# Split weight tiles and x tiles each followed by 16 unused bytes

## The chip, the cores and the metric

The kernel runs on one core of one Trainium2 chip. The metric is the device time of one execution, in microseconds (us). Three runs of the kernel before gave 2096.66, 2097.6 and 2097.91 us, median 2097.6 us.

## What is computed

One layer of a streaming encoder on 256 tokens of width 2048, in f32. Cut to its matrix products (names as in the kernel's stream):

```python
h = rmsnorm(x)                       # [256, 2048]
A, Z, GA..GC, BQK, BV, BO, CQK, CV = split(h @ w_in)       # three token mixers and their gates
x += (gate_a*(y_a@wb_a) + gate_b*(y_b@wb_b) + gate_c*(y_c@wb_c)) @ w_out     # BR, WO
q = rmsnorm(x) @ xa_wq;  k, v = split(rmsnorm(mem) @ xa_wkv)                 # Q, K, V
x += cross_attention(q, k, v) @ xa_wo                                        # XO
x += (silu(g) * u) @ ffn_down,  g, u = split(conv3(rmsnorm(x) @ ffn_up))     # UP, DN
```

The gated DeltaNet, the mLSTM and the stick-breaking attention between the products are not touched by the change.

## The kernel before, in words

Every large product is done in the format `float32r` with each operand split in two: a high part, the value rounded to that format, and a low part, the rest. Three matmuls replace one (function `three`, L1699): high weights by high x, high weights by low x, low weights by high x.

**Units and halves.** The stream (L43) cuts all weights into units of 256 columns. SyncE loads a unit into one of the two slots of `raw`. A unit is then worked on in two halves. ScalarE writes the high part of a half into `w_hi[:, half]` (L457, called from `hi_half`), VectorE writes `raw - w_hi` into `w_lo[:, half]` (L974, `lo_half`), and TensorE multiplies (`half_unit`, L1718). In the feature-major stages (kind FM and BR) a half is 16 blocks k of 128 rows by 128 columns, so 48 matmuls of 256 columns. The weights are the stationary operand there and x the moving one. In the down projection DN a half has 11 blocks, 33 matmuls. In UP (L1731 to L1737) the first two of the three products are one matmul of 512 columns, since the high and the low x are read in one access, so a half has 32 matmuls: 16 of 512 columns (L1735) and 16 of 256 (L1737). In the token-major stages BV, CV and V the roles are exchanged: x is stationary and 256 columns of weights move.

**Order.** TensorE takes the halves in the order of the stream. It waits for `lo_ready` before each, and ScalarE waits for `half_used` before it overwrites a half. Between the halves lie the smaller matmuls of the mixers and of the attention. The order is written out by hand.

**Where the tiles lie.** Tensors follow each other in each partition, each start rounded up to 32 bytes. In bytes modulo 128, counted from the start of `w_hi` (the place, below): `raw`, `w_hi` and `w_lo` have sizes that are multiples of 128, and so has a block of weights (512 bytes), so all blocks of weights lie at place 0. `x_home` starts at place 0 and the kernel puts x into it at a byte of its own for each use (L140): `x_hl` (all products with `w_in`) at 32, `x_wo` at 64, `x_q` at 96, `x_xo` at 16, `x_up` at 32. A block of x has 1024 bytes, and the low x lies 16384 bytes behind the high x, so the place is the same for all k and both parts. The tensors behind `x_home` add up so that `y_hl` (BR), `mem_hl` (K and V), `act_hl` (DN) and `gw_hi`, `gw_lo` (the four small gate matrices: 48 matmuls in the form of a half, after the first three halves of A) all lie at place 32.

In one table, with the relation, which is the place of the moving operand less that of the stationary one, modulo 128:

| products | moving | stationary | relation before |
|---|---|---|---|
| w_in, feature-major | x_hl, 32 | w, 0 | 32 |
| gate matrices | x_hl, 32 | gw, 32 | 0 |
| BR, K, DN | y_hl, mem_hl, act_hl, 32 | w, 0 | 32 |
| WO | x_wo, 64 | w, 0 | 64 |
| Q | x_q, 96 | w, 0 | 96 |
| XO | x_xo, 16 | w, 0 | 16 |
| UP | x_up, 32 | w, 0 | 32 |
| BV, CV, V | w, 0 | x_hl or mem_hl, 32 | 96 |

Of the kernel before, what the change touches and what calls it, by code (L numbers as in the profile page):

```python
# [8 lines left out]
P = 128  # L9
SEQ, D = 256, 2048  # L10
TT = SEQ // P
KC = D // P
# [7 lines left out]
CW = 256  # L20
# [95 lines left out]
def build_program(nc, T, out):  # L116
    f32, f32r = mybir.dt.float32, mybir.dt.float32r
    ALU, ACT, AX = mybir.AluOpType, mybir.ActivationFunctionType, mybir.AxisListType
    ctx = ExitStack()
    with ctx:  # L120
        def sb(name, shape, dt=f32, stack=ctx):
            return stack.enter_context(nc.sbuf_tensor(name, shape, dt))

        def sem(name):
            return ctx.enter_context(nc.semaphore(name))


        raw = sb("raw", [P, 2, KC * CW])
        w_hi = sb("w_hi", [P, 2, KC * P], f32r)
        w_lo = sb("w_lo", [P, 2, KC * P], f32r)  # L130
        e_scope = ExitStack()
        x_back = sb("x_back", [P, KC, SEQ], f32, e_scope)
        o_tm = sb("o_tm", [P, TT, D], f32, e_scope)
# [1 line left out]
        p_scope = ExitStack()  # L135
        prob = sb("prob", [P, TT, XH, SEQ], f32, p_scope)
        p_scope.close()
        x_home = sb("x_home", [P, 2 * KC * SEQ + 32], f32r)
        x_at = lambda byte: x_home[:, byte // 4:byte // 4 + 2 * KC * SEQ].rearrange("p (j k s) -> p j k s", j=2, k=KC)
        x_hl, x_wo, x_q, x_xo, x_up = (x_at(byte) for byte in (32, 64, 96, 16, 32))  # L140
        tmp = sb("tmp", [P, 2, 1024])
        ident = sb("ident", [P, P])
        upper = sb("upper", [P, P])
# [130 lines left out]
        y_hi, y_lo, br_c, br_m, m_hi, m_lo = (sem(n) for n in ("y_hi", "y_lo", "br_c", "br_m", "m_hi", "m_lo"))  # L274
# [3 lines left out]
        xl_t, xl_v, xl_a, xp_v, xp_t, xp_e, xo_t, xo_h, xo_l = (sem(n) for n in (  # L278
            "xl_t", "xl_v", "xl_a", "xp_v", "xp_t", "xp_e", "xo_t", "xo_h", "xo_l"))
# [75 lines left out]
        def halves(tile, kind, half, slot):  # L355

            if kind == TM_:
                return tile[:, slot, half * (KC // 2) * CW:(half + 1) * (KC // 2) * CW]
            k = DG if kind == DOWN else KC
            return tile[:, slot, 0:k * CW].rearrange("p (k n) -> p k n", n=CW)[:, :, half * P:(half + 1) * P]  # L360

        def split_out(tile, kind, half):
            if kind == TM_:
                return tile[:, half, :]
            k = DG if kind == DOWN else KC
            return tile[:, half, 0:k * P].rearrange("p (k n) -> p k n", n=P)


        @block.gpsimd
# [72 lines left out]
        def mb(i):  # L442
            return bank[4 + i % 4]
# [11 lines left out]
        def _(act):  # L455
            def copy(out_, in_, func=ACT.Copy, **kw):
                return nc.scalar.activation(out_, in_, func, **kw)  # L457
# [315 lines left out]

            def merged_hi(i, par):
                act.wait_ge(br_m, i + 1)
                copy(x_wo[:, 0, bass.ds(i * 2, 2), :].rearrange("p c s -> p (c s)"), tmp[:, par, 0:512]).then_inc(m_hi, 1)

            def br_unit(i, par, hp):
                hi_half("BR", i, par, hp, 0)
# [49 lines left out]

            def output_hi(c):  # L830
                act.wait_ge(xo_t, c + 1)
                copy(x_xo[:, 0, 2 * c:2 * c + 2, :].rearrange("p c s -> p (c s)"), mb(c)[:, :]).then_inc(xo_h, 1)

            m = first_half("V")
            hi_half(*half_of(m))
# [12 lines left out]
            for p in range(XH):  # L848
                beside(m + 3 + p)
                for a in range(TT):  # L850
                    j = 2 * p + a
# [86 lines left out]
            with act.Fori(1, D // CW) as c:  # L938
                for g in range(NDG):
                    par, h0 = slot_of("DN", g)  # L940
# [24 lines left out]
        def _(dve):  # L965
            v = nc.vector
            tt = v.tensor_tensor
# [277 lines left out]
            for l in range(7):  # L1245
# [17 lines left out]
                for g in range(3):  # L1263
# [5 lines left out]
                    for x, S_X in ((0, S_T), (1, S_U))[l // 6:]:  # L1269
                        t = level_columns(S_X[:, 4 * g:4 * g + 4, :], l, x)  # L1270
                        o = bank[2 + 2 * g + x][:, 0:4 * P // 2].rearrange("p (n b w) -> p n b w", n=4, w=1 << l)
# [28 lines left out]
            for g in range(3):  # L1300
                dve.wait_ge(a_t, 4 + g)
                t = S_L[:, 4 * g:4 * g + 4, :].rearrange("p c s -> p (c s)")
# [138 lines left out]

            def merged_lo(i, par):
                dve.wait_ge(m_hi, i + 1)
                two = lambda j: x_wo[:, j, bass.ds(i * 2, 2), :].rearrange("p c s -> p (c s)")
                tt(two(1), tmp[:, par, 0:512], two(0).bitcast(f32), ALU.subtract).then_inc(m_lo, 1)

            def br_unit(i, par, hp):
                lo_half("BR", i, par, hp, 0)
# [74 lines left out]

            def output_lo(c):
                dve.wait_ge(xo_h, c + 1)
                tt(x_xo[:, 1, 2 * c:2 * c + 2, :].rearrange("p c s -> p (c s)"), mb(c)[:, :],
                   x_xo[:, 0, 2 * c:2 * c + 2, :].rearrange("p c s -> p (c s)").bitcast(f32), ALU.subtract).then_inc(xo_l, 1)

            m = first_half("V")
            lo_half(*half_of(m))  # L1530
# [165 lines left out]
        def _(pe):  # L1696
            mm = nc.tensor.matmul
# [20 lines left out]
            def half_unit(name, i, par, hp, half, acts, ready=None):  # L1718

                kind = kind_of[name]  # L1720
                pe.wait_ge(lo_ready, hp * 4 + (2 * par + half + 1))
                if kind == TM_:
                    for k in range(KC // 2):
                        kk = half * (KC // 2) + k
                        w = [t[:, half, k * CW:(k + 1) * CW] for t in (w_hi, w_lo)]
                        for a in range(TT):
                            x = [acts[:, j, kk, a * P:(a + 1) * P] for j in range(2)]
                            last = three(bank[par + 2 * a][:, 0:CW], x, w, kk == 0, kk == KC - 1)
                else:
                    cuts = (0, GH, GH + MH, KC) if kind == BR else (0, KC)  # L1730
                    for k in range(KC if name == "UP" else 0):  # L1731
                        if ready and k % ready[2] == 0:
                            pe.wait_ge(ready[0], ready[1] + k // ready[2] + 1)
                        o = up_bank(par, half)
                        mm(o[:, :].rearrange("p (j s) -> p j s", j=2), w_hi[:, half, k * P:(k + 1) * P], acts[:, :, k, :],  # L1735
                           start=k == 0, stop=False)
                        last = mm(o[:, SEQ:2 * SEQ], w_lo[:, half, k * P:(k + 1) * P], acts[:, 0, k, :], start=False, stop=k == KC - 1)  # L1737
                    for k in range(0 if name == "UP" else KC):
                        if ready and k % ready[2] == 0:
                            pe.wait_ge(ready[0], ready[1] + k // ready[2] + 1)  # L1740
                        g = sum(k >= c for c in cuts) - 1
                        w = [t[:, half, k * P:(k + 1) * P] for t in (w_hi, w_lo)]
                        last = three(bank[par + 2 * g][:, half * SEQ:(half + 1) * SEQ], w, [acts[:, j, k, :] for j in range(2)],
                                     k == cuts[g], k + 1 == cuts[g + 1])
                last.then_inc(half_used, 1)
# [61 lines left out]
            for i, k in ((0, 74), (1, 72), (2, 88), (3, 88), (4, 88)):  # L1807
                last = nc.tensor.transpose(bank[4][:, at:at + k], vecs[0:k, i, :], ident[0:k, 0:k])
# [8 lines left out]
            for k in range(KC):  # L1817
                last = three(bank[4][:, 0:SEQ], [t[:, k, :] for t in (gw_hi, gw_lo)], [x_hl[:, j, k, :] for j in range(2)],
                             k == 0, k == KC - 1)
# [4 lines left out]
            for a in range(TT):  # L1824
                nc.tensor.transpose(bank[5][:, a * P:(a + 1) * P], rt[:, a * P:(a + 1) * P], ident[:, :])
                last = nc.tensor.transpose(bank[5][:, SEQ + a * MH:SEQ + (a + 1) * MH], rt2[:, a * P:(a + 1) * P], ident[0:MH, 0:MH])
# [44 lines left out]
            for j in range(3):  # L1871
                for x in range(2):
                    last = spread(mb6(j + 3)[:, x * SEQ:(x + 1) * SEQ], 2 * j + x, g_row[:, :])
# [6 lines left out]
            for g in range(6):  # L1880
                if g == 3:
                    pe.wait_ge(dec_v, 12)
                for c in range(2):
                    for a in range(TT):
                        last = nc.tensor.transpose(mb6(g)[:, (2 * c + a) * P:(2 * c + a + 1) * P], tm[:, a, 2 * g + c, :], ident[:, :])
# [7 lines left out]
            for l in range(7):  # L1893
# [4 lines left out]
                for g in range(3):  # L1898
                    ns = range(4 * g, 4 * g + 4)
                    if l:  # L1900
                        last = group(bank[5 + g], lambda n: S_C[:, n, :], lambda n: S_U[:, n, :], ns)
                    else:
                        for n in ns:
                            last = nc.tensor.transpose(bank[5 + g][:, n % 4 * P:n % 4 * P + P], S_C[:, n, :], ident[:, :])
# [270 lines left out]
            def down_pair(c, par):  # L2175
                if isinstance(c, int) and c < 2:
                    pe.wait_ge(dve_evac, evacuated("UP", COUNT["UP"] - 1)[1])
                else:
                    pe.wait_ge(dve_evac, c + (evacuated("DN", 0)[1] - 2))
                for g in range(NDG):  # L2180
                    for half in range(2):
                        pe.wait_ge(lo_ready, c * (2 * NDG) + (2 * FIRST["DN"] + 2 * g + half + 1))
                        for k in range(DG):
                            if isinstance(c, int) and c == 0 and g * DG + k == FC - 2:
                                pe.wait_ge(f_l, FC // 2)
                            w = [t[:, half, k * P:(k + 1) * P] for t in (w_hi, w_lo)]
                            x = [act_hl[:, j, g * DG + k, :] for j in range(2)]
                            last = three(bank[par + 2 * half][:, 0:SEQ], w, x, g + k == 0, g * DG + k == FC - 1)
                        last.then_inc(half_used, 1)
                    if g == 1 and not (isinstance(c, int) and c == 0):  # L2190
                        finished(c - 1, 1 - par)
# [41 lines left out]
```

## Time and profile before

| | |
|---|---|
| median of the runs | 2097.6 us |
| profiled execution, its own time | 2098.79 us |
| its span, from the first to the last instruction | 2096.6 us |
| mean granted TensorE clock | 0.992 |
| TensorE matmul busy | 2052.9 us, 98% |
| VectorE busy | 1229.7 us, 59% |
| ScalarE busy | 895.7 us, 43% |
| matmuls | 15803 |

The records of successive matmuls overlap, since a matmul is recorded from its start until its results are out. The busy time of a group of matmuls is therefore no measure of what it costs. What counts is the spacing, from one start to the next. It is read from a stretch that begins and ends with the start of a half: the view of stretches gives its length and the number of matmuls in it, and that number holds two that began before the stretch and were still under way, so the spacing is the length divided by the number less two. A column is one cycle: 256 columns at 2.4 GHz are 106.7 ns.

### The profile page before, as it was taken

To read this page: it belongs to the slowest core of one execution; us is meant where nothing else is said; L and a number is where in the kernel's file an instruction comes from. 1 tells how busy PE (TensorE), PEld (TensorE's weight loads), DVE (VectorE), ACT (ScalarE), POOL (GpSimd) and SP (SyncE) were. 2 spreads that over 40 slices of the span, in tenths; PEclk is the share of its full clock that TensorE was granted. 3 is DMA by queue.
4 is the path that set the end of the run, shared out by engine and by line. 5 is a ranking of instruction groups with operands and counts; after the bars stand their busy time and mean duration, and the time that the engine had idled before them with its cause. 6 is when DMAs were issued, how large, how long until landed. Compare 5 with 4: busy or idle time off the path is not lost.

```text
span 2096.6 us, 36640 instructions
## 1 busy us (share of the span) xinstructions
PE 2052.9 (98%) x15803; PEld 1983.2 (95%) x15803; DVE 1229.7 (59%) x1312; ACT 895.7 (43%) x864; POOL 34.0 (2%) x44
## 2 busy tenths in 40 slices
PE   5999999999999999999999999999999999999998
PEld 5999999999999999999999999888888888899998
DVE  5477644543544457577474445677877777744443
ACT  4444433344446443355444434544444444433332
POOL 2000000000000000000000000000000000000000
PEclk8999999999999999999999999999999999999999
DMA  7555444366455865656565355656555655556563
GB/s 220 162 177 190 137 133 134 111 205 200 151 172 176 299 198 189 213 161 190 177 194 163 121 160 166 218 178 200 188 179 193 200 181 180 181 199 194 188 195 125
DMA packets 358511, 377.43 MB, mean 180 GB/s; under 512 B 11913, under 2 KB 354723, under 8 KB 357123
## 3 DMA queue, kind: packets, MB, share of 16 engines
q1 hardware_dynamic: 354771, 353.36, 52.9%
q0 software_dynamic: 3632, 22.42, 2.9%
q8 instruction: 93, 1.52, 0.3%
q14 instruction: 15, 0.12, 0.0%
HBM read 364.75 MB, written 11.01 MB: 179 GB/s over the span
## 4 chain that ended last, share of the span: by engine, by line
PE 95%; DVE 2%; ACT 1%; issue 1%; DMA 0%; POOL 0%; SPq 0%; DVEq 0%; ACTq 0%
PE bank L1701 22%; PE bank L1703 22%; PE bank L1702 22%; PE bank L1735 15%; PE bank L1737 8%; PE bank L1912 1%; PE bank L1859 1%; DVE w_lo L974 1%; PE bank L2115 1%; PE bank L2096 1%; ACT w_hi L457 0%; DVE tmp L1018 0%; DVE x_home L1024 0%; PE bank L1846 0%; PE bank L1778 0%
## 5 line engine op out<-in xcount | busy, mean ns | idle before, releaser
L974 DVE TENSOR_TENSOR w_lo<-raw,w_hi 128x2048 fp32r<-128x2048 f32 (+1 forms) x352 | 763.8, 2170 | 630.3 <-ACT w_hi L457 629.8
L457 ACT ACTIVATE w_hi<-raw 128x2048 fp32r<-128x2048 f32 (+1 forms) x354 | 644.1, 1820 | 1105.8 <-PE bank L1703 827.3
L1701 PE MATMUL bank<-x_home,w_hi 128*128 128x256 f32 x2304 | 653.1, 283 | 18.3 <-DVE x_home L1024 15.2
L1703 PE MATMUL bank<-x_home,w_lo 128*128 128x256 f32 x2304 | 648.0, 281 | 0.0
L1702 PE MATMUL bank<-x_home,w_hi 128*128 128x256 f32 x2304 | 646.9, 281 | 0.0
L1735 PE MATMUL bank<-x_home,w_hi 128*128 128x512 f32 x1408 | 488.7, 391 | 3.6 <-DVE x_home L1583 2.2
L1701 PEld LDWEIGHTS bank<-x_home,w_hi 128*128 128x128 f32 x2304 | 436.2, 189 | 21.0 <-issue 13.3
L1702 PEld LDWEIGHTS bank<-x_home,w_hi 128*128 128x128 f32 x2304 | 437.0, 190 | 0.2
L1703 PEld LDWEIGHTS bank<-x_home,w_lo 128*128 128x128 f32 x2304 | 436.1, 189 | 0.0
L1737 PE MATMUL bank<-x_home,w_lo 128*128 128x256 f32 x1408 | 397.6, 282 | 0.0
L1735 PEld LDWEIGHTS bank<-x_home,w_hi 128*128 128x128 f32 x1408 | 264.4, 188 | 59.4 <-DVE xT L988 1.7
L1737 PEld LDWEIGHTS bank<-x_home,w_lo 128*128 128x128 f32 x1408 | 266.9, 190 | 0.0
L1701 PE MATMUL bank<-act_hl,w_hi 128*128 128x256 f32 x704 | 198.5, 282 | 3.9 <-issue 3.9
L1703 PE MATMUL bank<-act_hl,w_lo 128*128 128x256 f32 x704 | 198.0, 281 | 0.0
L1702 PE MATMUL bank<-act_hl,w_hi 128*128 128x256 f32 x704 | 197.9, 281 | 0.0
L1701 PEld LDWEIGHTS bank<-act_hl,w_hi 128*128 128x128 f32 x704 | 133.5, 190 | 4.2 <-issue 4.2
L1702 PEld LDWEIGHTS bank<-act_hl,w_hi 128*128 128x128 f32 x704 | 133.4, 190 | 0.0
L1703 PEld LDWEIGHTS bank<-act_hl,w_lo 128*128 128x128 f32 x704 | 133.4, 190 | 0.0
L1701 PE MATMUL bank<-w_hi,mem_hl 128*128 128x256 f32 x256 | 74.0, 289 | 0.0
L1623 DVE SCALAR_TENSOR_TENSOR tmp<-tmp,vec 128x254 f32<-128x254 f32 (+1 forms) x176 | 73.1, 479 | 0.0
L1702 PE MATMUL bank<-w_lo,mem_hl 128*128 128x256 f32 x256 | 72.0, 281 | 0.0
L1701 PE MATMUL bank<-mem_hl,w_hi 128*128 128x256 f32 x256 | 72.0, 281 | 0.0
(279 smaller groups left out, 2182.9 us busy)
## 6 DMA issues: line engine op xcount, KB each, us to landing
raw<-in_w_in SPq DMA_DIRECT2D x53, 2048.0 KB, 8.6
raw<-in_ffn_up SPq DMA_DIRECT2D x44, 2048.0 KB, 8.0
raw<-in_ffn_down SPq DMA_DIRECT2D x32, 1408.0 KB, 6.5
raw<-in_xa_wkv SPq DMA_DIRECT2D x16, 2048.0 KB, 8.9
raw<-in_w_br SPq DMA_DIRECT2D x8, 2048.0 KB, 8.3
raw<-in_w_out SPq DMA_DIRECT2D x8, 2048.0 KB, 8.7
raw<-in_xa_wq SPq DMA_DIRECT2D x8, 2048.0 KB, 8.1
raw<-in_xa_wo SPq DMA_DIRECT2D x8, 2048.0 KB, 8.1
```

Source lines behind the costliest of these rows:

```text
L457: return nc.scalar.activation(out_, in_, func, **kw)
L974: tt(split_out(w_lo, kind, half), halves(raw, kind, half, par), split_out(w_hi, kind, half).bitcast(f32), ALU.subtract).then_inc(lo_ready, 1)
L1623: ins = v.scalar_tensor_tensor(o, b, w, o, ALU.mult, ALU.add)
L1701: mm(o, w[0], x[0], start=start, stop=False)
L1702: mm(o, w[0], x[1], start=False, stop=False)
L1703: return mm(o, w[1], x[0], start=False, stop=stop)
L1735: mm(o[:, :].rearrange("p (j s) -> p j s", j=2), w_hi[:, half, k * P:(k + 1) * P], acts[:, :, k, :], start=k == 0, stop=False)
L1737: last = mm(o[:, SEQ:2 * SEQ], w_lo[:, half, k * P:(k + 1) * P], acts[:, 0, k, :], start=False, stop=k == KC - 1)
L1859: last = mm(o[:, i * P:(i + 1) * P], lhs(n), rhs(n), start=True, stop=True)
L1912: last = mm(bank[2 + 2 * g + x][:, n % 4 * 64:n % 4 * 64 + 64].rearrange("p (b w) -> p b w", w=1 << l), lhs[:, n, :], level_columns(rhs[:, ...
L2096: last = mm(mb(j)[:, 0:SEQ], qT[:, 4 * h + c, a * P:(a + 1) * P], kT[:, 4 * h + c, :], start=c == 0, stop=c == XC - 1)
L2115: last = mm(mb(c)[:, x * SEQ:(x + 1) * SEQ], v_tm[:, mk, f * P:(f + 1) * P], probT[:, mk, h, :], start=mk == 0, stop=mk == TT - 1)
```

## The change

The block of weights in `w_hi` and `w_lo` gets a step of 132 elements (528 bytes) in place of 128, and in the token-major stages a block of 256 columns gets 264 (1056 bytes). A block of x in `x_home` gets 260 elements (1040 bytes) in place of 256. All uses of `x_home` start at its first byte; the five starting bytes are gone. Each tensor grows: `w_hi` and `w_lo` by 512 bytes, `x_home` by 384, in all 1408, so whatever lies behind keeps its place modulo 128. Both parts of x and of the weights, and both halves, again lie a multiple of 128 bytes apart.

So block k of the weights lies at place 16k (32k in the token-major stages), and block k of x at place 16k. The relation of x to weights is 0 for every k in w_in, WO, Q, XO and UP. `y_hl`, `mem_hl`, `act_hl` and the gate matrices keep their layout, so their relation to the other operand changes by 16 bytes from block to block. No instruction, wait or transfer is added or removed. Some accesses of ScalarE and VectorE that ran through contiguous bytes now have 16 unused bytes after each 512, 1024 or (token-major) 1024 bytes.

```diff
+        WS = P + 4
+        CS = CW + 2 * 4
         raw = sb("raw", [P, 2, KC * CW])
-        w_hi = sb("w_hi", [P, 2, KC * P], f32r)
-        w_lo = sb("w_lo", [P, 2, KC * P], f32r)
+        w_hi = sb("w_hi", [P, 2, KC * WS], f32r)
+        w_lo = sb("w_lo", [P, 2, KC * WS], f32r)
...
-        x_home = sb("x_home", [P, 2 * KC * SEQ + 32], f32r)
-        x_at = lambda byte: x_home[:, byte // 4:byte // 4 + 2 * KC * SEQ].rearrange("p (j k s) -> p j k s", j=2, k=KC)
-        x_hl, x_wo, x_q, x_xo, x_up = (x_at(byte) for byte in (32, 64, 96, 16, 32))
+        XS = SEQ + 4
+        x_home = sb("x_home", [P, 2, KC, XS], f32r)
+        x_hl = x_home[:, :, :, 0:SEQ]
+        x_wo = x_q = x_xo = x_up = x_hl
...
         def split_out(tile, kind, half):
             if kind == TM_:
-                return tile[:, half, :]
+                return tile[:, half, 0:KC // 2 * CS].rearrange("p (k n) -> p k n", n=CS)[:, :, 0:CW]
             k = DG if kind == DOWN else KC
-            return tile[:, half, 0:k * P].rearrange("p (k n) -> p k n", n=P)
+            return tile[:, half, 0:k * WS].rearrange("p (k n) -> p k n", n=WS)[:, :, 0:P]
...
-                        w = [t[:, half, k * CW:(k + 1) * CW] for t in (w_hi, w_lo)]
+                        w = [t[:, half, k * CS:k * CS + CW] for t in (w_hi, w_lo)]
...
-                        mm(o[:, :].rearrange("p (j s) -> p j s", j=2), w_hi[:, half, k * P:(k + 1) * P], acts[:, :, k, :],
+                        mm(o[:, :].rearrange("p (j s) -> p j s", j=2), w_hi[:, half, k * WS:k * WS + P], acts[:, :, k, :],
                            start=k == 0, stop=False)
...
-                        w = [t[:, half, k * P:(k + 1) * P] for t in (w_hi, w_lo)]
+                        w = [t[:, half, k * WS:k * WS + P] for t in (w_hi, w_lo)]
```

The last edit stands twice, in `half_unit` and in `down_pair`. The writers of pairs of x blocks (`merged_hi`, `merged_lo`, `output_hi`, `output_lo`) write two rows of 256 where they wrote one of 512.

## Rows read from the trace of the kernel before

**Rows 1.** The page: busy time, share of the span and instructions of each engine

```profile
PE 2052.9 (98%) x15803; PEld 1983.2 (95%) x15803; DVE 1229.7 (59%) x1312; ACT 895.7 (43%) x864; POOL 34.0 (2%) x44
```

**Rows 2.** The page: the chain that ended last, by engine

```profile
PE 95%; DVE 2%; ACT 1%; issue 1%; DMA 0%; POOL 0%; SPq 0%; DVEq 0%; ACTq 0%
```

**Rows 3.** Waits by pair: us in total, times, longest us

```profile
ACT w_hi L457 <- PE bank L1703: 827.3, 249, 10.5
DVE w_lo L974 <- ACT w_hi L457: 629.8, 273, 9.1
ACT w_hi L457 <- PE bank L1737: 270.5, 87, 4.2
```

**Rows 4.** Order of time in UP: start us, us, engine, line, operation

```profile
1500.16 0.39 PE L1735 MATMUL bank<-x_home,w_hi 128*128 128x512 f32 x1
1500.16 0.19 PEld L1737 LDWEIGHTS bank<-x_home,w_lo 128*128 128x128 f32 x1
1500.39 0.28 PE L1737 MATMUL bank<-x_home,w_lo 128*128 128x256 f32 x1
1500.39 0.19 PEld L1735 LDWEIGHTS bank<-x_home,w_hi 128*128 128x128 f32 x1
```

**Rows 5.** Stretches, TensorE: from:to us, length, busy (matmuls), clock, DMA share, GB/s

```profile
57.23:62.98 5.75, 5.75 (x50) 1.00 1.01 320
62.99:91.24 28.25, 28.25 (x242) 1.00 0.47 149
131.98:182.37 50.39, 50.39 (x434) 1.00 0.63 200
677.02:738.60 61.58, 61.58 (x530) 1.00 0.87 301
749.98:839.57 89.59, 89.59 (x770) 1.00 0.58 188
846.92:875.16 28.24, 28.24 (x242) 1.00 0.77 262
937.96:960.99 23.03, 23.03 (x194) 1.00 0.61 195
968.36:1029.95 61.59, 61.59 (x530) 1.00 0.61 194
1083.48:1123.79 40.31, 40.31 (x338) 1.00 0.63 203
590.34:624.40 34.06, 34.06 (x290) 1.00 0.59 187
1252.54:1337.97 85.43, 85.43 (x722) 1.00 0.60 192
1393.39:1831.56 438.17, 438.17 (x2530) 1.00 0.58 188
1841.14:1884.68 43.54, 43.54 (x365) 1.00 0.54 174
```

**Rows 6.** The same view for two stretches of the steady loop of DN

```profile
1982.73:2009.67 26.94, 26.94 (x233) 1.00 0.64 205
2013.98:2040.90 26.92, 26.92 (x233) 1.00 0.66 205
```

**Rows 7.** Groups by shape in CV (592 to 622 us): busy us, mean ns | idle before

```profile
L457 ACT ACTIVATE w_hi<-raw 128x2048 fp32r<-128x2048 f32 x6 | 11.5, 1916 | 20.9 <-PE bank L1703 20.9
L974 DVE TENSOR_TENSOR w_lo<-raw,w_hi 128x2048 fp32r<-128x2048 f32 x6 | 13.8, 2292 | 20.2 <-ACT w_hi L457 20.2
```

**Rows 8.** The same view in GC (677 to 738 us)

```profile
L457 ACT ACTIVATE w_hi<-raw 128x2048 fp32r<-128x2048 f32 x11 | 21.1, 1919 | 35.7 <-PE bank L1703 31.5 <-DMA raw<-in_w_in 4.2
L974 DVE TENSOR_TENSOR w_lo<-raw,w_hi 128x2048 fp32r<-128x2048 f32 x11 | 25.2, 2293 | 36.8 <-ACT w_hi L457 36.8
```

**Rows 9.** Order of time in DN, ScalarE and VectorE: start us, us, line [idle before]

```profile
1990.63 1.38 ACT L457 ACTIVATE w_hi<-raw 128x1408 fp32r<-128x1408 f32 x1 [1.93 <-PE bank L1703]
1994.48 1.38 ACT L457 ACTIVATE w_hi<-raw 128x1408 fp32r<-128x1408 f32 x1 [2.47 <-PE bank L1703]
...
1988.25 1.62 DVE L974 TENSOR_TENSOR w_lo<-raw,w_hi 128x1408 fp32r<-128x1408 f32 x1 [2.28 <-ACT w_hi L457]
1992.04 1.63 DVE L974 TENSOR_TENSOR w_lo<-raw,w_hi 128x1408 fp32r<-128x1408 f32 x1 [2.17 <-ACT w_hi L457]
```

More of the change, by code:

```diff
@@ L357, in halves @@
             if kind == TM_:
-                return tile[:, slot, half * (KC // 2) * CW:(half + 1) * (KC // 2) * CW]
+                return tile[:, slot, half * (KC // 2) * CW:(half + 1) * (KC // 2) * CW].rearrange("p (k n) -> p k n", n=CW)
             k = DG if kind == DOWN else KC
@@ L775, in merged_hi @@
                 act.wait_ge(br_m, i + 1)
-                copy(x_wo[:, 0, bass.ds(i * 2, 2), :].rearrange("p c s -> p (c s)"), tmp[:, par, 0:512]).then_inc(m_hi, 1)
+                copy(x_wo[:, 0, bass.ds(i * 2, 2), :], tmp[:, par, 0:512].rearrange("p (c s) -> p c s", s=SEQ)).then_inc(m_hi, 1)
             def br_unit(i, par, hp):
@@ L831, in output_hi @@
                 act.wait_ge(xo_t, c + 1)
-                copy(x_xo[:, 0, 2 * c:2 * c + 2, :].rearrange("p c s -> p (c s)"), mb(c)[:, :]).then_inc(xo_h, 1)
+                copy(x_xo[:, 0, 2 * c:2 * c + 2, :], mb(c)[:, :].rearrange("p (c s) -> p c s", s=SEQ)).then_inc(xo_h, 1)
             m = first_half("V")
@@ L1443, in merged_lo @@
                 dve.wait_ge(m_hi, i + 1)
-                two = lambda j: x_wo[:, j, bass.ds(i * 2, 2), :].rearrange("p c s -> p (c s)")
-                tt(two(1), tmp[:, par, 0:512], two(0).bitcast(f32), ALU.subtract).then_inc(m_lo, 1)
+                two = lambda j: x_wo[:, j, bass.ds(i * 2, 2), :]
+                tt(two(1), tmp[:, par, 0:512].rearrange("p (c s) -> p c s", s=SEQ), two(0).bitcast(f32), ALU.subtract).then_inc(m_lo, 1)
             def br_unit(i, par, hp):
@@ L1525, in output_lo @@
                 dve.wait_ge(xo_h, c + 1)
-                tt(x_xo[:, 1, 2 * c:2 * c + 2, :].rearrange("p c s -> p (c s)"), mb(c)[:, :],
-                   x_xo[:, 0, 2 * c:2 * c + 2, :].rearrange("p c s -> p (c s)").bitcast(f32), ALU.subtract).then_inc(xo_l, 1)
+                tt(x_xo[:, 1, 2 * c:2 * c + 2, :], mb(c)[:, :].rearrange("p (c s) -> p c s", s=SEQ),
+                   x_xo[:, 0, 2 * c:2 * c + 2, :].bitcast(f32), ALU.subtract).then_inc(xo_l, 1)
             m = first_half("V")
@@ L1734, in half_unit @@
                         o = up_bank(par, half)
-                        mm(o[:, :].rearrange("p (j s) -> p j s", j=2), w_hi[:, half, k * P:(k + 1) * P], acts[:, :, k, :],
+                        mm(o[:, :].rearrange("p (j s) -> p j s", j=2), w_hi[:, half, k * WS:k * WS + P], acts[:, :, k, :],
                            start=k == 0, stop=False)
-                        last = mm(o[:, SEQ:2 * SEQ], w_lo[:, half, k * P:(k + 1) * P], acts[:, 0, k, :], start=False, stop=k == KC - 1)
+                        last = mm(o[:, SEQ:2 * SEQ], w_lo[:, half, k * WS:k * WS + P], acts[:, 0, k, :], start=False, stop=k == KC - 1)
                     for k in range(0 if name == "UP" else KC):
@@ L2185, in down_pair @@
                                 pe.wait_ge(f_l, FC // 2)
-                            w = [t[:, half, k * P:(k + 1) * P] for t in (w_hi, w_lo)]
+                            w = [t[:, half, k * WS:k * WS + P] for t in (w_hi, w_lo)]
                             x = [act_hl[:, j, g * DG + k, :] for j in range(2)]
```

## The prediction

> **What bounds the kernel now.** The page first: TensorE's matmuls are busy for 98% of the span, VectorE for 59%, ScalarE for 43% [rows 1], and TensorE holds 95% of the chain that ended last [rows 2]. The waits say the same from the other side: the longest is ScalarE's for TensorE to free a half of the weights (827.3 us in 249 waits, 270.5 us more in UP), then VectorE's for ScalarE [rows 3]. So the splitters stand ahead of TensorE and wait for it. Time is won or lost here only if one matmul follows another at a different spacing. The change alters no instruction, but it alters the addresses that TensorE reads.
>
> The order of time shows what TensorE does at once: the load of the next weights starts at the same moment as the matmul before it (1500.16 and 1500.16, 1500.39 and 1500.39) [rows 4]. Both read the same memory, so the relation of the two places can matter. The view of stretches shows whether it does. The length over the number less two gives the spacing of 256-column matmuls, against 106.7 ns of columns [rows 5]:
>
> - relation 32: 50.39/432 = 116.6 ns in A, 61.58/528 = 116.6 in GC, 89.59/768 = 116.7 in BR, 61.59/528 = 116.6 in K, 26.92/231 = 116.5 in DN [rows 6]; but 28.25/240 = 117.7 in early A, 23.03/192 = 119.9 in early K, 43.54/363 = 119.9 in early DN
> - relation 64 (WO): 28.24/240 = 117.7
> - relation 96 (Q): 40.31/336 = 120.0; with the roles exchanged (CV): 34.06/288 = 118.3
> - relation 16 (XO): 85.43/720 = 118.7
> - relation 0 (gate matrices): 5.75/48 = 119.8, between stretches of the same stage at 117.7
>
> The granted clock is 1.00 in all of them, and a DMA share of 0.87 beside 0.58 leaves GC and BR at the same spacing [rows 5], so neither clock nor DMA traffic makes the difference. The relation does, in part: Q differs from K by 3.4 ns for nothing but 64 bytes of place. Relation 32 also has more than one steady state, which a pause between halves can change.
>
> **The change part by part.** It moves all products with x from relations 32, 64, 96 and 16 to relation 0. The nearest row for it is the gate matrices' 119.8 ns, the only ones at that relation; its neighbours on the circle of 128 bytes, 16 (118.7) and 96 (120.0), enclose it, so I take 119.8. One difference: every third load belongs to the next block, so its relation is 0 less 16, which is 112, between 96 and 0, hence also near 119.9.
>
> 1. Products with w_in, feature-major: 96 halves of 48 matmuls. The first half runs at lower clock and is left out. 16 halves are in the state of 117.7, 79 in that of 116.6: 3792 x 3.2 ns = 12.1 us, and 768 x 2.1 ns = 1.6 us. Sum 13.7 us.
> 2. WO, 768 matmuls: 119.8 - 117.7 = 2.1 ns, 1.6 us. XO, 768: 1.1 ns, 0.9 us. Q, 768: -0.2 ns, -0.2 us. Sum 2.3 us.
> 3. UP, 1408 pairs of 512 and 256 columns: 438.17/1264 = 346.7 ns a pair [rows 5]. Its 768 columns are 320.0 ns, so each matmul carries 13.3 ns over its columns. That is what Q and early DN carry (120.0 - 106.7), the most that any stretch shows; the best carry 9.9. UP is already in the slowest state, so I take no change. Bounds: down to the best state, 6.8 ns a pair, -9.6 us; up by half as much, +4.8 us, since no row shows more than 13.3.
> 4. BR, K and DN keep their layout while the weights walk, so block by block their relation passes through all eight multiples of 16. By the rows the circle reads 119.8 (0), 118.7 (16), 116.6 (32), 117.7 (64), 120.0 (96), and between neighbours 117.2 (48), 118.9 (80), 119.9 (112): mean 118.6. BR: 768 x 1.9 = 1.5 us. K: 576 x 2.0 = 1.2, and the 192 early ones at 119.9 gain 0.2. DN: 2112 matmuls, of them 396 at 119.9 (-0.5 us) and 1716 at 116.6 (+3.4 us). Sum 5.4 us.
> 5. BV, CV and V, 1248 matmuls at 118.3: 118.6 by the same mean, 0.4 us.
> 6. ScalarE and VectorE. The nearest rows: the split of a half takes 1916 and 2292 ns where both sides are contiguous (CV) [rows 7] and 1919 and 2293 where the reading side jumps after each 128 elements (GC) [rows 8]. So a jump costs 1 to 3 ns in a whole access, and I take nothing for one on the writing side. The cover: in DN, where halves are shortest, ScalarE still waits 1.9 to 2.5 us before each half and VectorE 2.2 us [rows 9]. If the 16-byte shift slowed each split by a tenth (0.14 and 0.16 us), it would still be hidden; the chain of both has to grow by over a microsecond before TensorE waits. Bounds 0 and, without the cover, 0.3 us for each of the 64 halves of DN, 19 us, which I give no weight.
>
> Sum: 13.7 + 2.3 + 0 + 5.4 + 0.4 = 21.8 us, all on the path, since TensorE is the chain. The profiled execution took 2098.79 us, 2.2 above its span and 1.2 above the median of the runs. 2098.8 + 21.8 = 2120.6 us, by the median 2119.4 us. I forecast **2119.5 us**, 1.0% slower.
>
> One rule speaks against all of this. The rows above put 116.6 ns (K) beside 120.0 (Q) with the clock at 1.00 [rows 5]. The Trainium skill, page "TensorE: Matmul & The Clock Gate", section "Step-by-step: what each phase is for", says that TensorE has two independent read ports, and that loading the next weights takes no read bandwidth from the running matmul. By that rule places are of no account and the sum is 0. The trace disagrees: 64 bytes of place go with 3.4 ns a matmul. The rule stands behind the first rival.
>
> **The rivals.**
>
> - *No change, 2097.6 us (2094 to 2101).* The spacing would be a state that TensorE falls into when a stage starts, not a function of the relation. For it: relation 32 alone shows 116.6, 117.7 and 119.9, and the change from one to the other comes at a pause between halves, with all places as before. Against it: WO stays at 117.7, XO at 118.7 and Q at 120.0 over whole stages with several pauses each.
> - *Averaging, 2106.6 us (2102 to 2112).* A steady state needs places that stay; while they walk, every stage gets the circle's mean of 118.6. Then term 1 is 3792 x 2.0 + 768 x 0.9 = 8.3 us, WO +0.7, XO -0.1, Q -1.1, UP 2 x 1408 x -1.4 = -3.9, terms 4 and 5 5.8 as above: sum 9.7, less the part by which the gain in UP may be larger. For it: relation 32 is the only one that gave the best spacing, and no walk is in the trace. Against it: the relation in the products with x does stay, and nothing in the rows shows a cost of the absolute place.
> - *Faster, 2086 us (2080 to 2093).* Walking keeps TensorE out of the slow states, since a slow state needs the same meeting of the two reads again and again. All products with x, UP too, would run at the best spacing of 116.6: early A -0.8, WO -0.8, XO -1.6, Q -2.6, UP -9.6, together -15.4 us; half of term 4 and 5 stays, +3: 12 us faster. It decides at UP: unless a pair comes down from 346.7 towards 340 ns, there is no gain. For it: early K and early DN prove that 119.9 can become 116.6 without another place. Against it: the gate matrices at relation 0 were at 119.8 in a stage that before and after ran at 117.7.
>
> **How the numbers follow.** A difference of 0.2% (4.2 us) is about what a measurement of this kernel can tell from no change. Forecast 0.42, averaging 0.20, no change 0.15, faster 0.20, and 0.03 for a padding that costs more than the rows show. The forecast's own range is 2112 to 2127 us: relation 0 between 118.7 and 120.0 moves term 1 by 5 us, UP's upper bound adds 4.8. The range for 8 in 10 goes from 2085, inside the faster case, to 2127. Slower holds the forecast, nearly all of averaging and the rest: 0.63. Within 0.2%: 0.15. Faster: 0.22, with a part of "no change" that would lie beyond the bound.
>
> **What would show it.** In the stretches of the profile after: w_in's products at 119 to 120 ns from half to half (step 1; 116.6 makes it wrong, 118.6 is averaging); UP at 346 to 347 ns a pair (340 is the faster rival); BR and steady DN near 118.6 (step 4; 116.6 would mean that a walking relation costs nothing); splits of 1.92 and 2.29 us and no new wait of TensorE for VectorE (step 6). The prediction is wrong if w_in's products keep 116.6, whatever the rest does, since they hold two thirds of the sum.

## The result and the profile after

The changed kernel took 2109.66 us in the median of three runs (2109.15, 2109.66, 2113.02), against 2097.6 us. The ratio is 1.0062, 95% interval 1.0046 to 1.0079: 12 us slower. Its profiled execution took 2109.15 us, 10.4 us more than the one of before; its span is 2106.6 us, 10.0 us more.

The page after, its first part, again with TensorE as the bound [rows 1]:

```profile
PE 2063.7 (98%) x15803; PEld 1986.0 (94%) x15803; DVE 1229.9 (58%) x1312; ACT 896.5 (43%) x864; POOL 34.0 (2%) x44
```

Stretches of TensorE after, read as [rows 5]: the length over the number less two is the spacing. In order: gate matrices, A and Z, BQK, BR, WO, K, Q, XO, UP, early DN, steady DN.

```profile
56.83:62.47 5.64, 5.64 (x50) 1.00 1.02 321
131.81:182.97 51.16, 51.16 (x434) 1.00 0.62 198
421.54:467.02 45.48, 45.48 (x386) 1.00 0.66 209
752.46:842.91 90.45, 90.45 (x770) 1.00 0.58 186
850.25:878.68 28.43, 28.43 (x242) 1.00 0.78 263
971.79:1033.98 62.19, 62.19 (x530) 1.00 0.60 192
1092.52:1126.63 34.11, 34.11 (x290) 1.00 0.57 183
1255.06:1340.38 85.32, 85.32 (x722) 1.00 0.60 193
1396.18:1839.20 443.02, 443.02 (x2530) 1.00 0.58 186
1849.63:1892.45 42.82, 42.82 (x365) 1.00 0.52 167
1991.53:2014.86 23.33, 23.33 (x200) 1.00 0.64 197
```

The stages have become even. Products with x run at 118.4 ns (51.16/432), 118.5 in WO, 118.4 in Q, 118.5 in XO, where before they ran at 116.6, 117.7, 120.0 and 118.7. BR is at 117.8 and K at 117.8, from 116.7 and 116.6; early DN is at 118.0, from 119.9, and steady DN at 117.8, from 116.5. The gate matrices, where x walks now and the weights do not, went from 119.8 to 117.5. A pair in UP takes 350.5 ns (443.02/1264), from 346.7. The states that one stage had side by side are gone: of the halves of w_in's products that run without a pause, 56 of 58 lie at 118.5.

In UP the order of time (columns as [rows 4]) shows pairs of two kinds in turn. By the starts in ns, which the rows show rounded, block 0 takes 345 ns (from 1446.64) and block 1 takes 356 (from 1446.98), and so do even and odd blocks in the mean of all unbroken halves of UP; before, the means were 347 for both.

```profile
1446.64 0.39 PE L1738 MATMUL bank<-x_home,w_hi 128*128 128x512 f32 x1
1446.87 0.28 PE L1740 MATMUL bank<-x_home,w_lo 128*128 128x256 f32 x1
1446.98 0.40 PE L1738 MATMUL bank<-x_home,w_hi 128*128 128x512 f32 x1
1447.22 0.28 PE L1740 MATMUL bank<-x_home,w_lo 128*128 128x256 f32 x1
1447.34 0.39 PE L1738 MATMUL bank<-x_home,w_hi 128*128 128x512 f32 x1
```

Even and odd blocks differ, though their relation is the same. That points at the absolute place, but does not prove it: in Q of the kernel before, where nothing walks, the three matmuls of a block took 363 and 357 ns in turn. e7 decides it. ScalarE and VectorE are as before, and TensorE's waits for `w_lo` are too (2.9 us in all before, 2.5 after). Groups by shape in GC after (columns as [rows 7]):

```profile
L460 ACT ACTIVATE w_hi<-raw 128x2048 fp32r<-128x2048 f32 x10 | 19.2, 1920 | 32.2 <-PE bank L1706 28.2 <-DMA raw<-in_w_in 4.0
L977 DVE TENSOR_TENSOR w_lo<-raw,w_hi 128x2048 fp32r<-128x2048 f32 x10 | 22.9, 2293 | 30.1 <-ACT w_hi L460 30.1
```

By stage, from the first matmul of one to that of the next (us, before and after): w_in 718.2 and 720.3, BR 89.6 and 90.5, WO 98.4 and 98.7, K 92.0 and 92.3, Q 93.8 and 92.7, V 122.9 and 122.6, XO 93.0 and 92.9, UP 496.0 and 501.1, DN 261.0 and 263.4. In the first stage the changed spacing alone is worth 7.7 us (3792 x 1.9 and 768 x 0.7 ns), of which 2.1 show. Part of the difference is the clock: the profiled execution of before had two short spells at half the granted clock (0.50 from 202 to 205 us and from 376 to 378) there that the one after did not have. Stretches around them, before and then after:

```profile
195.00:215.00 20.00, 20.00 (x148) 0.91 0.37 120
370.00:385.00 15.00, 15.00 (x104) 0.89 0.43 140
```

```profile
195.00:215.00 20.00, 20.00 (x160) 1.00 0.38 121
370.00:385.00 15.00, 15.00 (x118) 1.00 0.39 123
```

Before both spells TensorE had just run twelve small matmuls of the mixers (`g_row`, L1846, 2.85 us). The execution after ran the same ones and stayed at 1.00. These spells come and go between executions, so the spacing, not the time, is what the single executions below are compared by.

### The profile page after: what moved, and what is told of

It is laid out like the page before. It is cut to its first block, busy times and chain, and to the rows that moved or that the text cites. A ratio compares the mean times of both kernels' runs of the same rounds, so it can differ in the third digit from the quotient of the medians.

```text
span 2106.6 us, 36640 instructions
## 1 busy us (share of the span) xinstructions
PE 2063.7 (98%) x15803; PEld 1986.0 (94%) x15803; DVE 1229.9 (58%) x1312; ACT 896.5 (43%) x864; POOL 34.0 (2%) x44
## 4 chain that ended last, share of the span: by engine, by line
PE 95%; DVE 2%; ACT 1%; issue 1%; DMA 0%; POOL 0%; SPq 0%; DVEq 0%; ACTq 0%
PE bank L1704 22%; PE bank L1705 22%; PE bank L1706 21%; PE bank L1738 15%; PE bank L1740 8%; PE bank L1915 1%; PE bank L1862 1%; DVE w_lo L977 1%; PE bank L2118 1%; PE bank L2099 1%; ACT w_hi L460 0%; PE bank L1775 0%; DVE tmp L1021 0%; DVE x_home L1027 0%; PE bank L1849 0%
## 5 line engine op out<-in xcount | busy, mean ns | idle before, releaser
L1738 PE MATMUL bank<-x_home,w_hi 128*128 128x512 f32 x1408 | 494.0, 396 | 3.5 <-DVE x_home L1586 2.2
L1704 PE MATMUL bank<-y_hl,w_hi 128*128 128x256 f32 x256 | 71.8, 281 | 0.0
```

The source lines that it names most:

```text
L1704: mm(o, w[0], x[0], start=start, stop=False)
```

## Experiments

Twelve kernels, in which only places in memory differ. Where no ratio is given the time is that of a single execution. The kernel before took 2097.8 us on the chip of e1 to e4, 2096.9 on that of e5 to e7, 2096.4 for e8 to e11 and 2097.4 for e12. Most were made to tell theory R (the spacing follows from the relation) from theories of places and walks. "Theory W" and "theory P" below are the same thought, first and second form: a walk takes the mean over the places it meets.

**e1: fixed, relation 0.** Is the changed kernel's 118.5 that of relation 0?

```diff
-        x_hl, x_wo, x_q, x_xo, x_up = (x_at(byte) for byte in (32, 64, 96, 16, 32))
+        x_hl, x_wo, x_q, x_xo, x_up = (x_at(byte) for byte in (0, 48, 80, 112, 0))
```

> The kernel before (nothing walks), with other starting bytes of x: w_in's products at relation 0, WO at 48, Q at 80, XO at 112, UP at 0; the places stay. Theory R (the spacing is a function of the relation alone): w_in's products at the 118.5 ns that the changed kernel shows at relation 0, UP at its 353.9 us per 1000 pairs, that is 350 to 354 ns a pair. Theory W (walking averages over places): a fixed relation 0 has a spacing of its own, 119.8 ns by the gate matrices of the kernel before, and not 118.5; UP likewise not that of the changed kernel. WO, Q and XO give three new points of the circle; by interpolation 117.2, 118.9 and 119.9 ns.

2116.6 us. Stretches of e1 in w_in, Q, XO and UP:

```profile
427.79:473.86 46.07, 46.07 (x386) 1.00 0.65 207
1102.50:1137.05 34.55, 34.55 (x290) 1.00 0.56 180
1271.02:1341.73 70.71, 70.71 (x626) 1.00 0.56 180
1397.64:1844.25 446.61, 446.61 (x2530) 1.00 0.57 182
```

w_in is at 120.0 ns and UP at 353.3 ns a pair: a fixed relation 0 is what the gate matrices had shown, and the same relation with the walk is faster. Theory R falls in its plain form. XO at relation 112 runs at 113.3 ns (70.71/624), which was not expected and is 3.3 below the best of the kernel before. WO (48) is at 118.3, Q (80) at 120.0.

**e2: the walk, with relation 32.**

```diff
-        x_home = sb("x_home", [P, 2, KC, XS], f32r)
+        x_room = sb("x_room", [P, 2 * KC * XS + 32], f32r)
+        x_home = x_room[:, 8:8 + 2 * KC * XS].rearrange("p (j k s) -> p j k s", j=2, k=KC)
```

> The changed kernel with x starting 32 bytes later: everything walks as there, but the relation in the products with x is 32 in place of 0. Theory R: w_in, WO, Q and XO at 116.6 ns, UP at 346.7 ns a pair; time about 2098 us. Theory W: they stay at 118.5 +- 0.3 ns, since the walk and not the relation sets them; time about 2110 us.

2106.1 us. Stretches of e2 in w_in and UP: 45.26/384 = 117.9 ns and 350.4 ns a pair.

```profile
422.00:467.26 45.26, 45.26 (x386) 1.00 0.66 210
1388.82:1831.74 442.92, 442.92 (x2530) 1.00 0.57 184
```

So the walk spoils relation 32 (116.7 fixed) by 1.2 ns while it mends relation 0 (120.0 fixed) by 1.5. That is as theory W wants it, but not quite: 117.9 is outside its 118.5 +- 0.3.

**e3: the weights alone walk.** The changed kernel with the x_home of before.

```diff
-        x_home = sb("x_home", [P, 2, KC, XS], f32r)
-        x_hl = x_home[:, :, :, 0:SEQ]
-        x_wo = x_q = x_xo = x_up = x_hl
+        x_home = sb("x_home", [P, 2 * KC * SEQ + 32], f32r)
+        ... (x_hl to x_up at bytes 32, 64, 96, 16, 32, as before)
```

> Only the weights are followed by 16 unused bytes; x lies as in the kernel before (32, 64, 96, 16, 32). The relation now changes from block to block everywhere. Theory W (average over what a walk meets): w_in, WO, Q and XO all at the 117.8 ns that BR and K show in the changed kernel, where also only the weights walk, whatever their starting bytes; time about 2101 to 2106 us. Theory R, taken block by block, expects the same 117.8. The two differ in UP: by the mean of the circle it is the same for any start.

2109.2 us, over the 2106 expected; its w_in stage had two low-clock spells (the stretches 190 to 215 and 365 to 385 us show clocks of 0.86 and 0.91). w_in 117.8, WO 117.7, Q 117.7 ns as expected, XO 118.3 (0.5 off), UP 349.6 ns a pair. A relation that changes from block to block gives nearly the same as one that stays, as long as something walks.

**e4: the weights fixed at byte 32.** A gap of 32 bytes ahead of `w_hi` and one of 96 behind `w_lo`.

```diff
+        gap = sb("gap", [P, 8])
         w_hi = sb("w_hi", [P, 2, KC * P], f32r)
         w_lo = sb("w_lo", [P, 2, KC * P], f32r)
+        gap2 = sb("gap2", [P, 24])
-... for byte in (32, 64, 96, 16, 32))
+... for byte in (32, 48, 0, 96, 64))
```

> The kernel before with the weights 32 bytes further (place 32, nothing walks), x_hl at 32, x_wo 48, x_q 0, x_xo 96, x_up 64: relations 0, 16, 96, 64, 32; BR, K and DN get relation 0. If only the relation counts: w_in as in e1 at relation 0, WO 118.7, Q 120.0, XO 117.7 ns, UP 346.7 ns a pair, BR, K and DN as w_in. If the absolute place counts too, at least one of them differs by over 0.5 ns.

2106.8 us. Stretches of e4 in w_in and XO:

```profile
424.37:469.93 45.56, 45.56 (x386) 1.00 0.66 208
1267.08:1337.79 70.71, 70.71 (x626) 1.00 0.57 181
```

w_in 118.6 (e1: 120.0), WO 118.6, Q 120.0, UP 346.7 as expected; XO 113.3 where 117.7 was expected. The gaps had moved x by 128 bytes against the weights. Counted modulo 256 the relations were 128, 144, 96, 192 and 160, so the deviating ones may need no absolute place, if the circle is larger than the 128 bytes by which the prediction counted. e6 and e8 bear on it.

**e5: everything at 112.** The same line as in e1 with (112, 112, 112, 112, 112).

> The kernel before with all five uses of x starting at byte 112 (nothing walks, relation 112). e1 showed XO there at 113.3 ns, the lowest so far. Theory R (spacing is set by the relation, whatever the stage): w_in, WO, Q and XO at 113.3 ns; against the kernel before 3792 x 3.3 + 768 x 4.5 + 768 x 4.5 + 768 x 6.7 + 768 x 5.4 ns = 28.5 us less, and UP at 340 ns a pair, 9.4 us less: about 2060 us. Rival S (XO is special as a stage): w_in stays over 116.6 ns, time over 2090 us.

2083.6 us, ratio 0.9943 (0.9926 to 0.9960). Stretches of e5 in w_in and UP:

```profile
412.86:456.37 43.51, 43.51 (x386) 1.00 0.68 216
1364.30:1810.91 446.61, 446.61 (x2530) 1.00 0.57 182
```

w_in, WO, Q and XO are all at 113.3, so it is the relation and not the stage. But UP went up, to 353.3 ns a pair, where 340 was expected: 9.4 us more in place of 9.4 us less. By stage (as above) w_in takes 705.7 us, 12.5 less where 16.0 were expected, Q 4.7 less, XO 4.0, WO 2.3, UP 9.1 more. A pair in which 512 columns move over one load follows another order of relations.

**e6: more fixed relations.** Starting bytes 192, 224, 144, 160 and 112, with x_home longer by 256 bytes.

> The kernel before with x_hl at byte 192, x_wo at 224, x_q at 144, x_xo at 160, x_up at 112; the weights at 0. Theory R256: the relation counts modulo 256 and not 128. It was read from e1 and e4, since in e4 all tensors behind the weights had also moved by 128: there x at 192 from the weights gave 113.3 ns while the kernel before gave 117.8 at 64. Expected: w_in 113.3 (192), WO 118.4 (224, as V), Q 118.65 (144, as e4's WO), XO 116.7 (160, by UP's 346.7), UP 340 (112). By a circle of 128 bytes: w_in 117.8 (64), WO 120.0 (96), Q 118.7 (16), XO 116.7 (32).

2101.2 us. Stretches of e6 in WO (224) and XO (160):

```profile
841.06:869.46 28.40, 28.40 (x242) 1.00 0.78 263
1251.17:1326.04 74.87, 74.87 (x626) 1.00 0.53 169
```

Half right. 224: 118.3 in WO, as in V and not 120.0 as at 96, and 144: 118.6. 192: 113.3 in 38 halves and 117.8, the value at 64, in 17 of them. 160: 120.0, where 116.7 was expected. UP at 112: 353.3, as e5. So 224 differs from 96, and a circle of 128 bytes does not fit. The other pairs can't tell: one relation can show several values (116.7, 117.8 and 120.0 at 32; 113.3 and 117.8 at 192), and 160 showed only 120.0, 64 only 117.8.

**e7: the weights fixed at byte 16.** Each weight tile becomes a view that starts 16 bytes into a tile 256 bytes longer; x at 16, 256, 224, 192 and 16.

```diff
-        w_hi = sb("w_hi", [P, 2, KC * P], f32r)
+        w_hi = sb("w_hi_room", [P, 2 * KC * P + 64], f32r)[:, 4:4 + 2 * KC * P].rearrange("p (j n) -> p j n", j=2)
```

> The weights start at byte 16 (nothing walks), x_hl at 16, x_wo 256, x_q 224, x_xo 192, x_up 16: relations 0, 240, 208, 176 and 0. Theory R: only the relation counts, so w_in at 120.0 ns and UP at 353.3 ns a pair, as in e1 where both began at 0. Then the changed kernel's 118.5 at relation 0 has to come from its every third pair (relation 240 there), and the walk as such does nothing. Theory P (places count, the walk averages over them): UP here at 346.9 ns a pair, so that the mean of the places 0 and 16 (353.3 and 346.9) is the changed kernel's 350.1, and w_in below 118.5.

2112.5 us. Stretches of e7 in w_in, BR and UP: 118.3 ns and 348.3 ns a pair in w_in and UP, against 120.0 and 353.3 in e1 at the same relation 0.

```profile
424.00:469.43 45.43, 45.43 (x386) 1.00 0.66 210
760.35:846.74 86.39, 86.39 (x722) 1.00 0.60 193
1395.38:1835.66 440.28, 440.28 (x2530) 1.00 0.58 185
```

So the absolute place counts. The mean of the two pairs, 350.8, is near the changed kernel's 350.5, but its parts do not fit: the changed kernel takes 345 ns in even blocks, where the fixed place (e1) gives 353.3, and 356 in odd ones, where it (e7) gives 348.3. In BR, whose y stayed at 32 and so got relation 16, the spacing is 120.0 (86.39/720), against the 118.7 of relation 16 with the weights at 0. The other relations of e7: 118.3 in WO (240), 117.8 in Q (208), 118.7 in XO (176).

**e8 and e9: the weights fixed at 32 and at 48.** As e7, with x at 32, 64, 144, 128, 32 and at 80, 48, 160, 96, 48.

> The weights start at byte 32 (nothing walks), x_hl at 32, x_wo 64, x_q 144, x_xo 128, x_up 32: relations 0, 32, 112, 96 and 0. Theory P (the absolute place counts, modulo 32): as in e1 with the weights at 0, w_in 120.0 ns (the gate matrices show it at 32 and 32), UP 353.3 ns a pair, WO 116.7, Q 113.3, XO 120.0. Theory P64 (modulo 64): some of these differ by over 0.5 ns.

> The weights start at byte 48 (nothing walks), x_hl at 80, x_wo 48, x_q 160, x_xo 96, x_up 48: relations 32, 0, 112, 48 and 0. Theory P modulo 32: as e7 with the weights at 16, so WO (relation 0) 118.3 ns and UP 348.2 ns a pair. Open, and wanted: w_in at relation 32 with the weights on an odd multiple of 16; if it lies at 118.5 to 119.5 in place of 116.7, the walk's 117.9 of e2 is the mean over even and odd places; if at 116.7, it is not. Q at relation 112 shows whether 113.3 holds at an odd place.

e8: 2130.1 us. w_in 120.0, UP 353.3, Q (112) 113.3, XO (96) 119.9; WO (32) 116.7 in 3 halves and 117.8 in 8. e9: 2106.7 us. Stretches of e8 in w_in, Q and UP, then of e9 in w_in, Q, XO and UP:

```profile
427.88:473.95 46.07, 46.07 (x386) 1.00 0.65 207
1103.28:1135.91 32.63, 32.63 (x290) 1.00 0.60 192
1402.79:1849.39 446.60, 446.60 (x2530) 1.00 0.57 182
```

```profile
421.91:467.33 45.42, 45.42 (x386) 1.00 0.66 209
1094.84:1128.91 34.07, 34.07 (x290) 1.00 0.57 181
1262.29:1335.08 72.79, 72.79 (x626) 1.00 0.54 174
1390.54:1830.85 440.31, 440.31 (x2530) 1.00 0.57 185
```

In e9 w_in (relation 32) is at 118.3, UP (0) at 348.3, WO (0) at 118.3 with two halves at 116.7, and Q (112) at 118.3 in eight halves and at 120 in the first four. Weight places that differ by 32 are alike at relation 0 (120.0 in e1 and e8, 118.3 in e7 and e9), places that differ by 16 are not: with the weights at an even multiple of 16 bytes relations 0, 32 and 112 give 120.0, 116.7 and 113.3, at an odd multiple 118.3. Relations 32 and 112 are good only at even places. Odd places have an order of their own: XO at relation 48 ran at 116.7 (72.79/624) in all its unbroken halves, against 118.3 for 48 in e1, and 16 was slow in e7.

Two readings more. The mean of even and odd places for relation 32 is 117.5, 0.4 below e2's 117.9. And e8 beside e4 excludes the circle of 128 bytes: the weights lie at 32 in both, x_hl lies 128 bytes further in e4, and w_in runs at 120.0 and 118.6.

**e10 and e11: the version that the experiments point to.** All x at 112, UP's at 32 (e10) or 192 (e11), and `y_hl`, `mem_hl` and `act_hl` brought to 112.

```diff
-... for byte in (32, 64, 96, 16, 32))
+... for byte in (112, 112, 112, 112, 32))
-        act_hl = sb("act_hl", [P, 2, FC, SEQ], f32r, d_scope)
+        act_hl = sb("act_hl_room", [P, 2 * FC * SEQ + 24], f32r, d_scope)[:, 20:20 + 2 * FC * SEQ].rearrange("p (j k s) -> p j k s", j=2, k=FC)
 (y_hl and mem_hl in the same way)
```

> Nothing walks; the weights at 0, all uses of x and also y_hl, mem_hl and act_hl at 112, UP's x at 32. Theory: relation 112 with the weights at 0 gives 113.3 ns in every stage. From e5 (2083.6 us): BR, K and DN from 116.7 to 113.3 ns (768 + 768 + 2112 matmuls, 396 of them in one run or another at 118 to 120) 12.5 us less, UP back to 346.7 ns a pair, 9.4 us less; V and its stationary mem_hl at another relation, +-1.5 us: 2062 us, between 2058 and 2067. Rival: 113.3 belongs to x_home and the others stay at 116.7: 2074 us.

> As e10, with UP's x at 192. e6 showed w_in at 113.3 ns in two thirds of its halves at relation 192. If UP's pair follows that, 340 ns and 9.4 us less than e10; if it does not, 346.7 to 353.3 ns and the same as e10 or 9 us more. The relations seen in UP so far: 346.7 at 32, 353.3 at 0 and 112.

e10: 2066.65 us, ratio 0.9852 (0.9835 to 0.9868), 30 us faster than the kernel before. Stretches of e10 in w_in, BR, Q, XO, UP and DN:

```profile
416.86:460.37 43.51, 43.51 (x386) 1.00 0.68 217
745.90:827.49 81.59, 81.59 (x722) 1.00 0.63 201
1069.23:1101.87 32.64, 32.64 (x290) 1.00 0.61 190
1237.08:1307.78 70.70, 70.70 (x626) 1.00 0.57 181
1363.09:1801.33 438.24, 438.24 (x2530) 1.00 0.58 186
1953.01:1975.44 22.43, 22.43 (x200) 1.00 0.67 205
```

The feature-major products run at 113.3 ns, UP at 346.7 ns a pair, DN at 22.43/198 = 113.3. After a lone gap of 200 ns in GA 5 to 13 matmuls follow at about 119 ns, at the same places, before 113.3 returns. The token-major stages, V among them, went to 120; the bound of 1.5 us had allowed for V. e11: 2075.5 us, ratio 0.9892 (0.9876 to 0.9909); UP at 353.3, so it follows relation 192 no more than 112.

**e12: the walk, with relation 112.** As e2, with 112 bytes.

> The changed kernel with x starting 112 bytes later: weights and x walk as there, relation 112. Fixed, relation 112 gave 113.3 ns with the weights on an even multiple of 16 bytes (e5, e8, e10) and 118.3 on an odd one (e9). Theory P (the walk takes the mean of even and odd places): w_in, WO, Q and XO at 115.8 ns, within 0.6 for every third pair, whose relation is 96. Theory R (the relation alone): 113.3. Theory of a walk that is indifferent to the relation: 118.2 +- 0.4, as in the changed kernel and e2. UP: about 350 ns a pair as in both. Time by theory P: 2109.7 less 4656 x 2.7 + 768 x 3 x 2.7 ns = 2091 us.

2110.6 us, ratio 1.0059 (1.0042 to 1.0076). Stretches of e12 in w_in and UP:

```profile
425.12:470.39 45.27, 45.27 (x386) 1.00 0.65 210
1392.20:1836.52 444.32, 444.32 (x2530) 1.00 0.56 183
```

117.9 ns and 351.5 ns a pair. Theory P fails: the mean of 113.3 and 118.3 is 115.8. Every third load, at relation 96, closes part of the 2.1 ns: at the 120.0 of that relation wherever it falls, the mean is (2 x 115.8 + 120.0)/3 = 117.2, an estimate. The walk gives 118.5, 117.9 and 117.9 at relations whose fixed values at even places are 120.0, 116.7 and 113.3. It is all but indifferent to the relation that it keeps.

## Why the prediction was right, and where it was not

The direction was right, and so was the premise under it: nothing but TensorE's spacing moved, by the addresses alone, while the splits of ScalarE and VectorE cost nothing. The size was too large, 21.8 us forecast and 12.1 measured in the medians. The time lies in the wide range (2085 to 2127) but below the forecast's own, 2112 to 2127, and inside that of averaging, 2102 to 2112.

The mechanism was right only in part. The forecast put 13.7 of its 21.8 us on relation 0, as if the value of places that stay held for places that walk. e2 keeps w_in's relation of 32 and walks: 117.9 ns. So of the step from 116.6 to 118.4 in w_in about 1.2 ns came with the walk and 0.6 with relation 0, and e2 as a whole was 8.3 us slower than the kernel before (single executions). By the prediction's own signs w_in's 118.5 was the mark of averaging (118.6). That the kernel became slower was forecast for a reason that holds for the smaller part of w_in; to that extent the sign was luck. Point by point:

1. *Step 1, w_in.* This is the term that was mis-sized: 119.8 ns was taken from the gate matrices, 118.5 measured. The row was read rightly as the value of relation 0 (e1, e8: 120.0), but it was one of places that stay. The prediction's own rival, averaging, had 118.6. Terms of 13.7 us forecast, 7.7 by the spacing, and in the stage 2.1. The two low-clock spells of the profiled execution before explain about 3.4 us of the difference (20 x 0.09 + 15 x 0.11, an estimate from the clocks); that the remaining 2.2 are hidden where TensorE waits for the mixers anyway is likely but was not measured. The third load was taken to be near 119.9 too, by interpolation at 112; fixed at 112, w_in runs at 113.3 (e5).
2. *Step 2, WO, XO, Q.* +2.3 us forecast, -1.0 measured (0.4, -0.2, -1.2). The same error: all three came to 118.5.
3. *Step 3, UP.* No change forecast, +5.1 us measured, just beyond the bound of +4.8. The premise that failed is that 13.3 ns over a matmul's columns, the most that any row showed, was UP's ceiling. A pair can carry 33.3 (353.3 less 320.0, e1, e5, e8) and not only 26.7, and UP's 346.7 was the best and not the worst value of the relations tried.
4. *Step 4, walking weights under fixed x.* +5.4 us forecast; BR +0.9, K +0.3, DN +2.4, together +3.6. The mean of the circle was 118.6, the measured value 117.8. That a walk costs something here was right. Part of the excess is the interpolation: the circle is not smooth, and 112, taken as 119.9 between its neighbours, measured 113.3. With the fixed values measured at even places (120.0, 118.7, 116.7, 118.3, 117.8, 120.0, 120.0, 113.3) its mean is 118.1.
5. *Step 5*, +0.4 forecast, V -0.3 measured. *Step 6*: 1920 and 2293 ns in GC against 1919 and 2293, as forecast.

Averaging came nearer than the forecast, in time (2106.6, 3.1 us off, against 9.8) and in w_in, but had the sign of UP wrong, and e12 speaks against its simplest form. "No change" and "faster" are excluded by the interval. By the Trainium skill's rule that the load of weights takes nothing from the running matmul's reads ("TensorE: Matmul & The Clock Gate", section "Step-by-step: what each phase is for") the places would be of no account. These runs do not bear that out: with the same matmuls the spacing goes from 113.3 to 120.0 ns with the places alone, and the kernel from 2066.65 us (e10) to 2130.1 (e8).

What stays open: why a walk of 16 bytes a block ends at 117.8 to 118.5 whatever the relation. It is not the plain mean of the fixed values at even and odd places (e12, and in UP not even block by block), and with each third load counted 0.7 of e12's 2.1 ns are still missing. One relation can show several values (113.3 and 117.8 in e6; 116.7, 117.8 and 119.9 in the kernel before), and in e10 a gap is followed by some slower matmuls at the same places, so something beside the places counts. That it is the time at which load and matmul meet is argued, not shown. So is the cause as a whole, a collision of the two reads; no record shows a collision. A circle of 128 bytes is excluded (120.0 and 118.6 in e8 and e4, 120.0 and 118.3 at 96 and 224); whether it has 256 was not tested. The changed kernel moved `y_hl`, `mem_hl`, `act_hl` and the gate matrices by 1408 bytes, which is 128 modulo 256. That did not matter for BR: e2, which lacks this shift, has it at the same 117.8.

## What to carry to other kernels

Where matmuls run back to back and each has its own weight load, compare their spacing between stages before anything else: equal instructions at unequal spacing point at addresses. Hold the places of both operands fixed in every block, scan the starting byte of the moving operand in steps of 16 in one run with another start for each stage, and check matmuls of another width by themselves. Look at every half of a stage and not at one stretch, since one place can show several values. The padding tried here, which moves the places by 16 bytes from block to block, evens the spacing out and gives up the best one.

## What the runs showed of the hardware

- The spacing of 256-column f32r matmuls with a load of 128 columns each takes the values 113.3, 116.7, 117.8, 118.3, 118.7 and 120.0 ns with nothing changed but the starting byte of the operands, at a granted clock of 1.00 (2.4 GHz), where the columns alone are 106.7. Some starts show more than one of them.
- Relation 112 with the weights at an even multiple of 16 bytes gave 113.3 ns in each of seven stages in which it was tried (w_in, BR, WO, K, Q, XO, DN; e5 and e10); at an odd multiple (Q in e9) 118.3 and 120. At an odd multiple relation 48 gave 116.7 (XO in e9) and 118.3 at an even one (WO in e1).
- Pairs of 512 and 256 columns took 346.7 ns (relations 32, 160), 353.3 (0, 112, 192), and 348.3 with the weights at an odd multiple (0).
- Sixteen unused bytes after each 512 on the writing side cost ScalarE and VectorE nothing that shows (1920 and 2293 ns, from 1919 and 2293). In the token-major stages, where there are 32 after each 1024, the splits took 1919 and 2293 ns (CV), from 1916 and 2292.
